# RWKV doubling steps: the transposed X taken from a transpose of the new X on PE, ScalarE's copies in another order

## The reference, cut to what matters

```python
def step(s, inp):
    r_t, w_t, k_t, v_t, kk_t, a_t = inp
    sa = jnp.einsum('bhij,bhj->bhi', s, -kk_t)
    s = s * w_t[:, :, None, :] + sa[..., None] * (kk_t * a_t)[:, :, None, :] + v_t[..., None] * k_t[:, :, None, :]
    return s, jnp.einsum('bhij,bhj->bhi', s, r_t)
```

## Time and profile before

| | us |
|---|---|
| median of 3 runs | 2720.31 (2718.95 to 2721.55) |
| the profiled execution's own time | 2721.9 |
| its span in the trace | 2720.0 |
| PE busy | 2604.2 (96% of the span) |
| DVE busy | 1738.1 (64%) |
| ACT busy | 1259.8 (46%) |
| POOL busy | 815.3 (30%) |
| mean granted TensorE clock | 0.988 |

### The profile page before, as it was taken

One profiled execution on the slowest core, in us unless ns is written; L12 is line 12 of the kernel. 1 busy time (PEld: TensorE's weight loads), 2 busy tenths in 40 slices (PEclk: granted clock), 3 DMA queues, 4 the chain that ended last, 5 costly groups with the idle time before them and its releaser, 6 DMA issues.

```text
span 2720.0 us, 57389 instructions
## 1 busy us (share of the span) xinstructions
PE 2604.2 (96%) x18602; PEld 2453.3 (90%) x18602; DVE 1738.1 (64%) x3107; ACT 1259.8 (46%) x2301; POOL 815.3 (30%) x612
## 2 busy tenths in 40 slices
PE   7989988888999999999999999999999999999998
PEld 7989977888999999999999999999988888888876
DVE  4467964333664564558986688778866666666656
ACT  5446532223444444544445543444445555555545
POOL 0021014333000000038988887777730000000000
PEclk9999989999999999999999999999999999999999
DMA  6655530000565556665555555555555565666664
GB/s 203 184 163 163 172 124 1 1 0 0 150 184 163 175 173 180 176 172 178 178 174 173 169 164 158 158 160 157 157 176 192 193 193 193 193 193 192 193 224 162
DMA packets 334661, 429.17 MB, mean 158 GB/s; under 512 B 26885, under 2 KB 299639, under 8 KB 333175
## 3 DMA queue, kind: packets, MB, share of 16 engines
q1 hardware_dynamic: 334583, 428.12, 51.4%
HBM read 423.82 MB, written 4.19 MB: 157 GB/s over the span
## 4 chain that ended last, share of the span: by engine, by line
PE 60%; issue 26%; POOL 10%; DVE 2%; DMA 1%; ACT 1%; POOLq 0%; SPq 0%; DVEq 0%; ACTq 0%
POOL w_lo L1060 9%; PE PS L370 8%; PE PS L371 8%; PE PS L372 8%; PE PS L695 8%; PE PS L696 8%; PE PS L697 8%; PE PS L659 2%; PE PS L534 1%; PE PS L498 1%; PE PS L532 1%; PE PS L523 1%; DVE w_lo L1074 1%; DMA raw<-in_peer_v 0%; PE PS L546 0%
## 5 line engine op out<-in xcount | busy, mean ns | idle before, releaser
L370 PE MATMUL PS<-act_hi,w_hi 128*128 128x256 f32 x4256 | 1218.1, 286 | 30.6 <-DVE w_lo L1074 16.9
L371 PE MATMUL PS<-act_lo,w_hi 128*128 128x256 f32 x4256 | 1207.8, 284 | 0.0
L372 PE MATMUL PS<-act_hi,w_lo 128*128 128x256 f32 x4256 | 1207.6, 284 | 0.0
L1074 DVE TENSOR_TENSOR w_lo<-raw,w_hi 128x512 fp32r<-128x512 f32 x1064 | 720.5, 702 | 308.2 <-ACT w_hi L723 304.9
L1060 POOL TENSOR_TENSOR w_lo<-raw,w_hi 128x512 fp32r<-128x512 f32 x512 | 669.3, 1340 | 675.6 <-ACT w_hi L918 675.6
L370 PEld LDWEIGHTS PS<-act_hi,w_hi 128*128 128x128 f32 x4256 | 819.8, 193 | 37.1 <-issue 19.5
L723 ACT ACTIVATE w_hi<-raw 128x512 fp32r<-128x512 f32 x1064 | 637.7, 624 | 417.0 <-PE PS L372 412.6
L371 PEld LDWEIGHTS PS<-act_lo,w_hi 128*128 128x128 f32 x4256 | 820.1, 193 | 1.0 <-issue 1.0
L372 PEld LDWEIGHTS PS<-act_hi,w_lo 128*128 128x128 f32 x4256 | 819.8, 193 | 0.0
L695 PE MATMUL PS<-w_hi,act_hi 128*128 128x512 f32 x1024 | 399.8, 390 | 3.8 <-DVE w_lo L1074 3.8
L696 PE MATMUL PS<-w_lo,act_hi 128*128 128x512 f32 x1024 | 399.5, 390 | 0.0
(11 more groups left out here) (243 smaller groups left out, 1684.4 us busy)
## 6 DMA issues: line engine op xcount, KB each, us to landing
raw<-in_peer_u SPq DMA_DIRECT2D x1024, 128.0 KB, 2.7
raw<-in_peer_v SPq DMA_DIRECT2D x256, 512.0 KB, 4.2
raw<-in_w_in SPq DMA_DIRECT2D x180, 512.0 KB, 3.8
raw<-in_w_out SPq DMA_DIRECT2D x32, 512.0 KB, 3.5
raw<-in_peer_w_q SPq DMA_DIRECT2D x128, 128.0 KB, 3.2
raw<-in_w_ret_branch SPq DMA_DIRECT2D x16, 512.0 KB, 3.5
raw<-in_w_rwkv_branch SPq DMA_DIRECT2D x16, 512.0 KB, 3.5
big<-in_x SPq DMA_DIRECT2D x2, 1024.0 KB, 5.9
```

The costliest lines, as they stand in the source:

```text
L370: pe.matmul(out, wh, xh, start=start, stop=False)
L371: pe.matmul(out, wh, xl, start=False, stop=False)
L372: return pe.matmul(out, wl, xh, start=False, stop=stop)
L1074: dve.tensor_tensor(w_lo[:, slot % 2, cols], raw[:, slot, cols], w_hi[:, slot % 2, cols].bitcast(f32), ALU.subtract).then_inc(S["unit_spli ...
```

## The change

On PE, step 4 is cut in two. For g = 0 and then g = 1 only the new X is made (at lv 4 only the new transposed X, as before), with the increment of `xx{g}`. Then, at lv 0 to 3, for g = 0 and then g = 1, PE waits for the copy of the new X and transposes it into bank 4g+3, with a second increment of `xx{g}`. L523 of the next level waits for the copy of X alone. L532 waits for the copy of the old `Xt` as well as for `wn{g}`. On ACT the two copies of X come first, then the two copies of `Xt`. `xx{g}` counts nine to a pass instead of five.

```diff
                         pe.wait_ge(S[f"lm{g}"], i * 5 + lv + 1)
-                        if lv == 0:
-                            pe.wait_ge(S[f"xc{g}"], i * 10 + 1)
-                        else:
-                            pe.wait_ge(S[f"xc{g}"], i * 10 + 2 * lv + 1)
+                        pe.wait_ge(S[f"xc{g}"], i * 10 + max(1, 2 * lv))
                         for n in range(4):
                             last = pe.matmul(PS[:, b + 1, n * P:(n + 1) * P], Lm[g][:, n, :], X[g][:, n, :], start=True, stop=True)
                         last.then_inc(S[f"w{g}"], 1)
@@
                         pe.wait_ge(S[f"wn{g}"], i * 5 + lv + 1)
-                        if lv < 4:
-                            for n in range(4):
-                                pe.matmul(PS[:, b + 2, n * P:(n + 1) * P], Xt[g][:, n, :], Wn[g][:, n, :], start=True, stop=True)
+                        pe.wait_ge(S[f"xc{g}"], i * 10 + 2 * lv + 1)
                         for n in range(4):
-                            last = pe.matmul(PS[:, b + 3, n * P:(n + 1) * P], Wn[g][:, n, :], Xt[g][:, n, :], start=True, stop=True)
+                            if lv < 4:
+                                last = pe.matmul(PS[:, b + 2, n * P:(n + 1) * P], Xt[g][:, n, :], Wn[g][:, n, :], start=True, stop=True)
+                            else:
+                                last = pe.matmul(PS[:, b + 3, n * P:(n + 1) * P], Wn[g][:, n, :], Xt[g][:, n, :], start=True, stop=True)
+                        last.then_inc(S[f"xx{g}"], 1)
+                    for g in range(2 if lv < 4 else 0):
+                        b = 4 * g
+                        pe.wait_ge(S[f"xc{g}"], i * 10 + 2 * lv + 2)
+                        for n in range(4):
+                            last = pe.transpose(PS[:, b + 3, n * P:(n + 1) * P], X[g][:, n, :], ident)
                         last.then_inc(S[f"xx{g}"], 1)
@@ scalar
                 for lv in range(5):
                     for g in range(2):
-                        act.wait_ge(S[f"xx{g}"], i * 5 + lv + 1)
                         if lv < 4:
+                            act.wait_ge(S[f"xx{g}"], i * 9 + 2 * lv + 1)
                             act.activation(X[g], PS[:, 4 * g + 2, :].rearrange("p (n c) -> p n c", n=4), ACT.Copy).then_inc(S[f"xc{g}"], 1)
+                    for g in range(2):
+                        act.wait_ge(S[f"xx{g}"], i * 9 + min(2 * lv + 2, 9))
                         act.activation(Xt[g], PS[:, 4 * g + 3, :].rearrange("p (n c) -> p n c", n=4), ACT.Copy).then_inc(S[f"xc{g}"], 1)
```

## The result

| | before | after |
|---|---|---|
| median of 5 runs, us | 2720.31 (2717.36 to 2721.55) | 2705.49 (2702.88 to 2711.01) |
| ratio | | 0.995 (95% interval 0.9936 to 0.9965) |
| the profiled execution's own time, us | 2721.9 | 2711.01 |
| its span, us | 2720.0 | 2709.1 |

The changed kernel is faster by 14.8 us in the medians; the forecast was 13.7. Its profiled execution was the slowest of its five, so the trace shows a little less gain than the medians do.

The account below looks back on a forecast made before the run. PE's stream alone was taken to set the recurrence's pace (28.1 of 29.7 us busy in one pass). Gains of 3.43 us a pass, 13.7 in four, took the median from 2720.31 to 2706.6 us, range 2704 to 2711.5.

Parts of the forecast that it names:

- The hole and the pitch: PE, doubling levels: 0.6 us hole before the second L523 goes; groups of four products keep a pitch of 0.89 us.
- The transpose group, 0.43 us: PE, doubling: four transposes at 0.106 us each take 0.43 us, replacing a product group of 0.89.
- The rival with a group at 0.89: PE, doubling: transposes between products cost like products; level gains 0.40 us, all passes 6.4, giving 2713.9 us; chance 7%.
- The schedule of a level, 5.11 us: Doubling levels 1 to 3: PE's order, load by load, gives 5.11 us instead of 5.97, gain 0.86.
- The release of 0.05 us: Doubling: PE's next load comes 0.05 us after the engine it waits for ends; 0.12 us kept for the range.
- Level 0, 5.38: First doubling level, second L523 held by POOL's mask: 5.38 us instead of 5.62, gain 0.24.
- Level 4, 3.72: Last doubling level, without a transpose: 3.72 us from L523 to L539 instead of 4.33, gain 0.61.
- The sum: Doubling: 0.24 + 3 x 0.86 + 0.61 = 3.43 us a pass, 13.7 us in four passes.
- "This gain needs the two changes together.": Levels 1 to 3: if L523 still waited for `Xt`, the copy ending at 5.97 would come after 5.11.
- Nothing meets it later: After the recurrence: SyncE's next transfer waits 281 us for a DVE split, so what follows moves with the stage's end.
- The held-up W product: Doubling level's end: next level's ready L523 g0 is held behind the second transpose by order alone, within a 0.46 us wait.
- The clock: PE, doubling: stays at 2.4 GHz; rival has it fall to half, near 2767 us if in all levels, chance 3%.

Follow-up runs that it names:

- e9: Changed kernel with each transpose of the doubling made twice; level 5.51 us, pass 26.10, median 2714.6 us, ratio 0.998 to the kernel before.
- e6: Changed kernel with PE's four passes written out instead of looped; level 5.07 us, pass 24.35 at i = 0, 2704.5 us in one run.
- e2: Changed kernel, but the W product (L523) waits again for the copy of `Xt`; level 5.23 us, median 2708.1 us, ratio 0.995 to the kernel before.
- e3: Changed kernel with ACT's copies back in the old order (X, `Xt` group by group); level 6.01 us, median 2722.5 us, ratio 1.0006 to before.
- e4: Changed kernel with each group's next-level W product put in front of its transposes; level 4.57 us, median 2697.8 us, ratio 0.9926 to before.
- e7: Changed kernel with each of L479's 16 transposes, behind PE's idle stretch, made eight times; 2717.7 us in one run.
- e8: Changed kernel with each transpose of L512, at a pass's start, made 24 times; 2773.9 us in one run.
- e1: Changed kernel with the transposed X again made by the old product, new order and relaxed wait kept; level 5.51 us, median 2714.3 us, ratio 0.998 to before.
- e10: Changed kernel with next W behind each group's transposed-X step, that step again the old product; level 5.51 us, median 2714.6 us, ratio 0.998 to before.
- e5: Changed kernel with each group's next-level W product right behind its transposes; level 4.60 us, median 2698.3 us, ratio 0.9911 to before.

## Why the prediction was right

- *The hole and the pitch.* As put: the hole of 0.6 us is gone, and the pitch of a product group stayed at 0.89.
- *The transpose group, 0.43 us.* Measured 0.107 x 4 between products (e9). The rival with a group at 0.89 is refuted by the level of 5.06. What I held against it was reckoned wrongly: for a group at 0.89 the one turn that lies on the path, from the second transpose group to the next product, would have to cost 0.46 us, over four transposes and not two.
- *The schedule of a level, 5.11 us.* Measured 5.06 in the written-out pass and 5.14 in the loop. The single steps agree: X at 1.94, transposes at 446.93 - 443.15 = 3.78 and 4.68, next level at 5.06. The last step, 0.38 instead of 0.43 us, is the term that I had too large. Behind a wait a group's first load starts together with its first transpose (both at 447.83), while the load of the next L520 runs 0.11 us ahead of its product (448.21 and 448.32). So from load to load the group takes 0.38 us.
- *The release of 0.05 us.* It held where waits are on constants. In the loop it was 0.13 behind DVE; e6 ties that to the loop, and the cause within it stays open. I had put this into the range, at up to 0.1 us a level; it was 0.07.
- *Level 0, 5.38.* Measured 503.98 - 498.64 = 5.34. *Level 4, 3.72.* Measured 462.08 - 458.36 = 3.72, and 3.79 in the loop.
- *The sum.* 3.43 us a pass forecast, 3.58 measured at i = 0 and 3.30 to 3.32 in the loop, 13.50 in all for the 13.7 forecast.
- *"This gain needs the two changes together."* Here the prediction read its own schedule wrongly. The copy that ends at 5.97 is that of group 1, and group 1's W product can't start before 5.11 + 0.89 = 6.00. e2, with the old wait, kept all but 1.3 us of the 13.5.
- *The hole's cause.* The prediction put it to the wait for `Xt`, and by the row under e2 that wait alone could have closed most of it in the old order. The sum didn't depend on which part closes it, so this had no test in the forecast.
- *Nothing meets it later.* The stretch behind the recurrence differs by 0.2 us.
- *ACT's order.* I wrote that it costs nothing. e3 shows the other side: without it there is no gain at all. The schedule had this in it, but the prediction did not say what the old order would have cost.
- *The held-up W product.* The prediction named it; e4 shows that it is 2.0 us a pass at i = 0.
- *The clock.* In the profiled execution the rival didn't come about inside the doubling, and the argument from the earlier trace rows is what e7 and e8 show. In other profiles the clock did fall in a level 0, in one or two of the four passes, at a cost of 1.2 to 1.4 us each (last section). The price of that rival left out level 4, which by the same rate would have added some 3.6 us a pass. By the rule of the Trainium skill ("TensorE: Matmul & The Clock Gate", Part 4: PE-mode transpose), that transposes don't engage the full clock, e7 would have stayed at 0.50; the measurement decides against it for these float32 transposes. But the mark that I set, a clock of 1.00 from 420 us on, was missed by four to five microseconds: in the changed kernel's profile the clock came back at 424.6 us, in that of the kernel before at 419.9. It cost the profiled execution 1.4 us, and stood in no term of my sum.

The forecast of the profiled execution, 2708.2 us, was met less well (2711.0) than that of the median (2706.6 for 2705.5). That the latter lies within 1.1 us is partly luck, since the single runs of this kernel scatter by 8. The firm confirmation is that of the passes, 13.50 us for 13.7.

## What to carry to other kernels

Write the schedule of one period out, load by load, with four durations from the trace: issue pitch, time to the reader, reader, release. It gave the level of the changed kernel and of e1 to e6, e9 and e10 within 0.1 us; the pass of e4 it missed by 0.45. A cheaper instruction on a full engine gives its saving only if the order can fill the wait that it opens: the same transposes were worth 1.8 us a pass in one order and 3.7 in another. On an engine with time to spare, the order of its queue can still be worth the whole gain. And before a gain is given to a new order, the relaxed wait alone should be priced in the old one: here the rows give it the same 1.8 us a pass.

## What the runs showed of the hardware that I had not expected

At the start of a pass PE has transposes with gaps, and waits for DVE and POOL. In some executions the clock was at half there for 2 to 4 us: in e1, e4 and e9 at i = 1, in e6 and e7 at i = 3, in e5 at i = 1 and 3; in the profiles of the kernels before and after, of e2, e3, e8 and e10 at none. Two windows of e4, with the clock third from the right:

```profile
492.00:494.00 2.00, 0.88 (x7) 0.49 (x5) 1.20 (x2) 1.48 (x3) 1.98 (x2) 1.00 0.00 0
...
496.00:498.00 2.00, 2.00 (x11) 2.00 (x11) 0.78 (x2) 0.00 (x0) 1.32 (x2) 0.50 0.00 0
```

The pass of e4 in which this falls takes 23.56 us instead of 22.27, so it costs 1.3 us; in e6 it is 25.63 instead of 24.35, in e7 25.92 instead of 24.56. Since e8 shows that transposes hold the clock up, the gaps are the likelier cause (PE was busy for 0.88 of 2.00 us before the fall). But no run here took them away alone, and the kernel before had the same kind of gaps without a fall (0.68 of 2.00 us in the earlier trace rows); why it befalls one pass and not another stays open. Each fall costs 1.2 to 1.4 us. It may be a part of the changed kernel's scatter of 8 us over five runs, but only one of these was profiled, and that one had no such fall.
